# A two-block transformer kernel on one core: the second attention's output with values stationary, its softmax division folded into the head norm

## What is computed

```python
scores = jnp.where(valid, scores + bias, -jnp.inf)
probs = jax.nn.softmax(scores, axis=-1)
out = jnp.einsum('bhcqk,bhckd->bhcqd', probs, vb)
...
y = group_rmsnorm(jnp.concatenate([y_sb, y_ch, y_cv], axis=-1), out_norm_w[l])
x = x + y @ w_out[l]

def group_rmsnorm(y, w):
    yg = y.astype(jnp.float32).reshape(b, s, N_OUT_GROUPS, HEAD_DIM)
    yg = yg * lax.rsqrt(jnp.mean(yg * yg, axis=-1, keepdims=True) + EPS)
    return (yg.reshape(b, s, D_MIX) * w.astype(jnp.float32)).astype(y.dtype)
```

## Time and profile before

| what | value |
|---|---|
| median of 3 runs | 691.27 us (691.0 to 691.66) |
| profiled execution, whole | 691.82 us |
| its span, first to last instruction | 689.9 us |
| TensorE busy | 682.8 us (99%) |
| VectorE busy | 485.6 us (70%) |
| ScalarE busy | 416.6 us (60%) |
| GpSimd busy | 90.7 us (13%) |
| mean granted TensorE clock | 0.997 of full |

### The profile page before, as it was taken

The page is one execution under the profiler, slowest core; times in us unless marked ns, Lnnn a source line. Parts: engine busy times, 40 slices in busy tenths (PEclk is TensorE's granted clock), DMA queues, the critical chain, the costliest instruction groups (busy, mean ns, idle before and its releaser), DMA issues.

```text
span 689.9 us, 9453 instructions
## 1 busy us (share of the span) xinstructions
PE 682.8 (99%) x3796; PEld 587.5 (85%) x3796; DVE 485.6 (70%) x739; ACT 416.6 (60%) x705; POOL 90.7 (13%) x164
## 2 busy tenths in 40 slices
PE   9999999999999999999999999999999999999996
PEld 8888888888888888888888988888888888888885
DVE  6878796767666666667465767777868877777774
ACT  7787775656555555546555866665567665555553
POOL 2122020688100000012700000000000000000001
PEclk9999999999999999999999999999999999999998
DMA  9936534736555555536434335554453565555401
GB/s 336 392 132 229 198 123 160 266 133 243 187 188 190 204 198 194 183 131 225 175 134 161 123 123 201 195 194 179 161 207 146 218 209 182 183 185 187 179 0 62
DMA packets 19484, 126.14 MB, mean 183 GB/s; under 512 B 2416, under 2 KB 2544, under 8 KB 5232
## 3 DMA queue, kind: packets, MB, share of 16 engines
q1 hardware_dynamic: 19296, 125.34, 49.9%
q10 hardware_dynamic: 144, 0.20, 0.1%
HBM read 124.48 MB, written 1.05 MB: 182 GB/s over the span
## 4 chain that ended last, share of the span: by engine, by line
PE 99%; DVE 0%; issue 0%; ACT 0%; POOLq 0%; POOL 0%
PE bank L222 96%; PE bank L231 3%; DVE xres L243 0%; POOLq L1572 0%; DVE last L243 0%; ACT last L234 0%; ACT junk L234 0%; POOL ss L248 0%; POOL ones L267 0%; POOL half L267 0%; POOLq L151 0%; POOLq L1640 0%
## 5 line engine op out<-in xcount | busy, mean ns | idle before, releaser
L243 DVE TENSOR_TENSOR wlo<-raw,whi 128x1024 fp32r<-128x1024 f32 x222 | 271.6, 1235 | 61.5 <-ACT whi L234 58.4
L234 ACT ACTIVATE whi<-raw 128x1024 fp32r<-128x1024 f32 x222 | 230.3, 1051 | 5.7 <-PE bank L222 3.8
L222 PE MATMUL bank<-xb,whi 128*128 128x512 f32 x496 | 124.2, 392 | 0.0
L222 PE MATMUL bank<-xa,whi 128*128 128x512 f32 x432 | 108.2, 392 | 0.0
L222 PEld LDWEIGHTS bank<-xb,whi 128*128 128x128 f32 x496 | 90.4, 188 | 17.4 <-DVE sg L243 0.2
L222 PE MATMUL bank<-whi,xb 128*128 128x512 f32 (+1 forms) x352 | 96.0, 355 | 0.0
L222 PEld LDWEIGHTS bank<-xa,whi 128*128 128x128 f32 x432 | 78.9, 188 | 15.5
L222 PEld LDWEIGHTS bank<-xb,wlo 128*128 128x128 f32 x496 | 67.7, 190 | 4.9
L222 PEld LDWEIGHTS bank<-whi,xb 128*128 128x128 f32 x352 | 62.1, 189 | 9.3 <-ACT vtok L234 0.3
L222 PE MATMUL bank<-xb,wlo 128*128 128x256 f32 x496 | 69.1, 282 | 0.0
L222 PEld LDWEIGHTS bank<-xa,wlo 128*128 128x128 f32 x432 | 58.9, 190 | 4.2
(11 more groups left out here) (263 smaller groups left out, 930.1 us busy)
## 6 DMA issues: line engine op xcount, KB each, us to landing
raw<-in_w_dram SPq DMA_DIRECT2D x109, 1024.0 KB, 4.8
first<-in_first_dram SPq DMA_DIRECT2D x8, 388.0 KB, 6.8
raw<-in_w_dram SPq DMA_DIRECT2D x4, 512.0 KB, 9.6
bias<-in_bias_dram SPq DMA_DIRECT2D x1, 1024.0 KB, 8.9
xres<-in_x_dram SPq DMA_DIRECT2D x1, 1024.0 KB, 8.1
gain<-in_ffn_norm_w_dram SPq DMA_DIRECT2D x1, 512.0 KB, 8.9
gain<-in_mix_norm_g_dram SPq DMA_DIRECT2D x1, 512.0 KB, 9.6
gain<-in_ffn_norm_g_dram SPq DMA_DIRECT2D x1, 512.0 KB, 4.8
```

Source lines behind the costliest of these rows:

```text
L222: return P(lambda e: e.matmul(o, l, r, start=start, stop=stop), *w, inc=inc)
L234: return A(lambda e: e.activation(o, i, f, **kw), *w)
L243: return q(lambda e: e.tensor_tensor(out=o, in0=a, in1=b, op=op), *w)
```

## The change

`ch_out` now takes a pair of heads at once: the values of a head are stationary (64 columns), the transposed weights move (256 columns for key block 0, 128 for key block 1), and the two heads write the lower and the upper 64 partitions of the bank. The result has features on partitions. It isn't divided by `den` any more. `finish` and `ch_finish` are gone; both groups use `feature_norm`.

Since the undivided output is `den` times the true one, its norm is the same if EPS is replaced by EPS times `den` squared. So `ch_den_squares` makes `den2` = EPS * den * den on VectorE, `ch_den_rows` transposes it on TensorE (two transposes to 8 rows of 256 tokens), splits it into `den_h` and `den_l`, and `ch_den_sums` adds it into the bank of the squared sums by matmuls with a selection matrix `sel_r` of eight rows, which GpSimd writes once during the first attention. The logarithm then has no bias. `ch_probs` transposes its three blocks in another order.

```diff
+    den2 = N("den2", [128, 16])
+    den_h, den_l = [at(va_at + 1024 * i, f"den{p}", [8, 256], F32R) for i, p in enumerate("hl")]
+    sel, sel_r = at(qta_at, "sel", [8, 512]), at(sbmask_at, "sel_r", [8, 512], F32R)
...
-    def feature_norm(y, ybank, kt, ytoks, sbank, f, hl, z, *free):
+    def feature_norm(y, ybank, kt, ytoks, sbank, f, hl, z, *free, more=None):
...
-            mm(pb[sbank][:, :], blk_r[:, :], l[:, :], False, True)
+            mm(pb[sbank][:, :], blk_r[:, :], l[:, :], False, more is None)
+            if more:
+                more()
...
     def ch_out(h):
-        bank, pt, c, o = 2 + h // 4, wk[4 + h % 4], slice(h * 64, h * 64 + 64), (h % 4) * 64
-        o0, o1 = pb[bank][:, o:o + 64], pb[bank][:, 256 + o:256 + o + 64]
-        mm(o1, pt[:, 0:128], vb[:, 0, c], True, False, ch["pT", h], *ch["v"], *bank_free[bank])
-        mm(o1, pt[:, 128:256], vb[:, 1, c], False, True)
-        ch["out", h] = [mm(o0, pt[:, 256:384], vb[:, 0, c], True, True, inc=True)]
...
+        bank, c0 = 2 + h // 4, 256 * (h // 2 % 2)
+        for k in range(2):
+            for i in range(2):
+                v, pt = vb[:, k, (h + i) * 64:(h + i) * 64 + 64], wk[4 + (h + i) % 4]
+                mm(pb[bank][64 * i:64 * i + 64, c0 + 128 * k:c0 + 256], v, pt[:, 256 * k:256 + 128 * k], k == 0, k == 1,
+                   ch["pT", h + i], *ch["v"], *bank_free[bank])
+        ch["out", h] = ch["out", h + 1] = [P.mark()]
+
+    def ch_den_squares():
+        d = den[:, :].rearrange("p (g t h) -> p g t h", g=2, t=2)
+        o = den2[:, :].rearrange("p (t g h) -> p g t h", g=2, t=2)
+        for g in range(2):
+            ch["den"] = stt(o[:, g], d[:, g], EPS, d[:, g], ALU.mult, ALU.mult, ch["e", 7])
+
+    def ch_den_rows():
+
+        P.wait(ch["den"], *bank_free[4])
+        for t in range(2):
+            tr(pb[4][0:8, t * 128:t * 128 + 128], den2[:, 8 * t:8 * t + 8])
+        p = P.mark()
+        a = copy(den_h[:, :], pb[4][0:8, 0:256], p)
+        v = low(den_l[:, :], pb[4][0:8, 0:256], den_h[:, :], a)
+        bank_free[4] = [v]
+        ch["den rows"] = [a, v]
+
+    def ch_den_sums(g, bank):
+        P.wait(*ch["den rows"], sel_tok)
+        for i in range(2):
+            s, o = sel_r[:, (2 * g + i) * 128:(2 * g + i) * 128 + 128], pb[bank][:, 256 * i:256 * i + 256]
+            mm(o, s, den_h[:, :], False, False)
+            mm(o, s, den_l[:, :], False, i == 1)
...
+    later(ch_den_squares)
     conv_taps(1)
     conv_unit(4)
+    ch_den_rows()
     ch_out(4)
-    ch_out(5)
...
     conv_unit(5)
-    ch_scaled_0()
     ch_out(6)
-    ch_out(7)
-    ch_roots, ch_scaled_1, ch_finish_1 = ch_finish(1)
-    later(ch_roots)
-
+    sums_0()
+    later(scaled_0)
+    later(split_0)
...
+    def other_squares():
+        squares_1(*ch["sums 0"])
+        cv_squares()
+    ch["sums 0"] = [P.mark()]
+    later(other_squares)
     for k in range(KT - HOLD):
         u, lh, ll, w = mix_1(k)
         out_unit(u, (0, 1), lh, ll, k == 0, False, *w)
         release(u)
-        if k == 0:
-            ch_finish_0()
-        elif k == 1:
+        if k == 1:
+            sums_1()
             cv_sums()
-            ch_scaled_1()
-            later(cv_scaled)
-            later(cv_split)
-        elif k == 2:
-            ch_finish_1()
+            for fn in (scaled_1, split_1, cv_scaled, cv_split):
+                later(fn)
```

More of the change, by code:

```diff
@@ L526, in two_block_program @@
     qa = N("qa", [128, 2, 512])
+    va_at = N.lo
     va = N("va", [128, 2, 256])
@@ L538, in two_block_program @@
     bias = N("bias", [128, 8, 256])
+    sbmask_at = N.lo
     sbmask = N("sbmask", [128, 3, 128])
@@ L562, in two_block_program @@
     den = N("den", [128, 16])
-    rden = N("rden", [128, 16])
+    den2 = N("den2", [128, 16])
+    den_h, den_l = [at(va_at + 1024 * i, f"den{p}", [8, 256], F32R) for i, p in enumerate("hl")]
+    sel, sel_r = at(qta_at, "sel", [8, 512]), at(sbmask_at, "sel_r", [8, 512], F32R)
     cva = at(qb_at, "cva", [128, 2, 256])
@@ L700, in sb_out, with squares @@
         sb["out", 2 * b] = sb["out", 2 * b + 1] = [P.mark()]
-    def feature_norm(y, ybank, kt, ytoks, sbank, f, hl, z, *free):
+    def feature_norm(y, ybank, kt, ytoks, sbank, f, hl, z, *free, more=None):
         (h, l), parts, summed, v = hl, [], [], []
-        def squares():
+        def squares(*read):
             a = act(f, y, ACT.Square, *ytoks, *free, scale=0.125)
-            parts.append(copy(h[:, :], f, a))
+            parts.append(copy(h[:, :], f, a, *read))
             parts.append(low(l[:, :], f, h[:, :], parts[0]))
@@ L712, in sums @@
             mm(pb[sbank][:, :], blk_r[:, :], h[:, :], True, False)
-            mm(pb[sbank][:, :], blk_r[:, :], l[:, :], False, True)
+            mm(pb[sbank][:, :], blk_r[:, :], l[:, :], False, more is None)
+            if more:
+                more()
             summed.append(P.mark())
         def scaled():
-            a = act(f, pb[sbank][:, :], ACT.Ln, *summed, eps_tok, bias=eps[:, 0:1])
+            a = act(f, pb[sbank][:, :], ACT.Ln, *summed, eps_tok, **({} if more else {"bias": eps[:, 0:1]}))
             bank_free[sbank] = [a]
@@ L732, in feature_norm @@
         return squares, sums, scaled, split
-    finishes = [0]
     sq_free, ytok = {0: [], 1: []}, {}
[L738 to L771, removed]
     ch = {}
@@ L827, in ch_probs @@
         P.wait(ch["e", h], *bank_free[bank])
-        for i in range(3):
-            tr(pb[bank][:, i * 128:i * 128 + 128], s[:, i * 128:i * 128 + 128])
+        for c, i in enumerate((2, 0, 1)):
+            tr(pb[bank][:, c * 128:c * 128 + 128], s[:, i * 128:i * 128 + 128])
         p = P.mark()
@@ L835, in ch_out @@
     def ch_out(h):
-        bank, pt, c, o = 2 + h // 4, wk[4 + h % 4], slice(h * 64, h * 64 + 64), (h % 4) * 64
-        o0, o1 = pb[bank][:, o:o + 64], pb[bank][:, 256 + o:256 + o + 64]
-        mm(o1, pt[:, 0:128], vb[:, 0, c], True, False, ch["pT", h], *ch["v"], *bank_free[bank])
-        mm(o1, pt[:, 128:256], vb[:, 1, c], False, True)
-        ch["out", h] = [mm(o0, pt[:, 256:384], vb[:, 0, c], True, True, inc=True)]
-    def ch_finish(g):
-        v = V(lambda e: e.reciprocal(rden[:, g * 8:g * 8 + 8], den[:, g * 8:g * 8 + 8]), ch["e", 4 * g + 3])
-        return finish(2 + g, 2 + 2 * g, ch["out", 4 * g + 3][0], 8 * g, v)
+        bank, c0 = 2 + h // 4, 256 * (h // 2 % 2)
[25 more added lines that the diff above has]
+            mm(o, s, den_l[:, :], False, i == 1)
     cv = {}
@@ L957, in two_block_program @@
             sb_squares()
+            g = memset(sel[:, :], 0.0, P.mark())
+            g = select(sel[:, :].rearrange("p (j d) -> p j d", d=64), [[-1, 8], [0, 64]], ALU.not_equal, 1.0, 0, 1, g)
+            sel_tok = G(lambda e: e.tensor_copy(sel_r[:, :], sel[:, :]), g)
         elif n == 2:
@@ L982, in two_block_program @@
     ch_out(0)
-    ch_out(1)
     ch_probs(2)
@@ L989, in two_block_program @@
     ch_out(2)
-    ch_out(3)
-    ch_roots, ch_scaled_0, ch_finish_0 = ch_finish(0)
-    later(ch_roots)
+    squares_0, sums_0, scaled_0, split_0 = feature_norm(
+        pb[2][:, :], 2, 2, ch["out", 2], 0, sq[0][:, :], sb_hl, yt[0][:, :], *sq_free[0], more=lambda: ch_den_sums(0, 0))
+    later(squares_0)
     ch_probs(4)
@@ L1003, in two_block_program @@
     conv_unit(5)
-    ch_scaled_0()
     ch_out(6)
-    ch_out(7)
-    ch_roots, ch_scaled_1, ch_finish_1 = ch_finish(1)
-    later(ch_roots)
+    sums_0()
+    later(scaled_0)
+    later(split_0)
+    squares_1, sums_1, scaled_1, split_1 = feature_norm(
+        pb[3][:, :], 3, 4, ch["out", 6], 0, sq[1][:, :], sb_hl, yt[1][:, :], *sq_free[1], more=lambda: ch_den_sums(1, 0))
     cv_squares, cv_sums, cv_scaled, cv_split = feature_norm(
-        flat(cvy[:, :, :]), None, 6, [cv["out"]], 0, cvf[:, :], cv_hl, flat(cvy[:, :, :]))
-    later(cv_squares)
+        flat(cvy[:, :, :]), None, 6, [cv["out"]], 1, cvf[:, :], cv_hl, flat(cvy[:, :, :]))
     us = next_units(KT)
```

## The result

| | median | lowest to highest | runs |
|---|---|---|---|
| before | 691.22 us | 691.0 to 691.66 | 6 |
| changed | 696.52 us | 696.03 to 698.05 | 6 |

The ratio is 1.0079, with a 95% interval of 1.0069 to 1.0089: 5.3 us slower. The forecast was 694.3, the range 693.0 to 697.3. The profiled execution of the changed kernel took 697.27 us (span 694.4) against 691.82 (span 689.9).

What follows compares the result with a forecast made beforehand. TensorE, 99% of the span, was taken as the bound. Work -6.01 + 5.27, stall 3.4, convolution wait 0.05 and held units 0.35 gave +3.06 us, so 694.3 us from the median of 691.27; range 693.0 to 697.3.

Steps and rivals of the forecast that it cites:

- the case that it stood for: Main forecast, chance 0.68: stall behind `conv_unit(4)` without a clock fall, 694.3 us.
- the forecast's own bounds: Main case's limits: 693.3 (work -1.0, stall 3.0, tail 0) to 696.8 us (work +0.2, stall 4.3, tail 1.0).
- the clock case: Rival, chance 0.12: the stall behind `conv_unit(4)` brings back TensorE's half rate, adding 3.0 us, 697.3 us.
- the prediction's own signs of being wrong: `den2` on VectorE before 88 us, `ch_out` over 1.2 us a pair, or 512-column matmuls behind the gap over 0.4 apart.
- The new wait: TensorE behind `conv_unit(4)` waits for VectorE's `den2`: a stall of 3.4 us, ends 3.0 and 4.3.
- The three microseconds of the earlier trace: At kernel start, 6 us of matmuls at the lower clock would be 3 less at full speed; priced the clock rival.
- The work of TensorE: Across the second attention and its norms: 6.01 us removed, 5.27 added, 0.74 gained, between 1.0 gained and 0.2 lost.
- What is late next: Norms behind the second attention: group 0 hidden, group 1 with 0.25 us to spare, the convolution's squares 0.05 us of waiting.
- The held units: Weight units on VectorE ahead of the residual sum delay TensorE's transposes of `xn`: 0.35 us added, ends 0 and 1.0.
- the long chain of sizes: Operations priced by size (0.6 to 0.72, 0.95, 1.13 us) put VectorE free 0.6 us after the residual sum could begin.
- That the wait is hidden: Rival: VectorE has the squared sums ready before `conv_unit(4)` ends, 690.9 us; chance 0.08 together with half the stall gone.
- The tail: Rival, chance 0.12: norms and held units each fall short if ScalarE runs 0.6 later, about 1.2 more, 695.5 us.

Runs made afterwards that it cites:

- the second profile: Changed kernel measured once more, unedited, beside the other runs: 696.73 us, ratio 1.0073 to the kernel before.
- the version without a gap: Changed kernel with `den2`'s two small operations ahead of VectorE's weight unit and their transposes behind head 7's probabilities: 692.16 us against 691.46 for the kernel before.
- the eight runs of the kernel before with a gap of 2.3 or 2.9 us: Kernel before plus one TensorE wait behind `conv_unit(4)`, for VectorE's row sum (696.59 us) or the weight unit's remainder (696.12 us), four runs each.
- the first profile: Profiled execution of the changed kernel from its first measurement: 697.27 us, against 691.82 for the kernel before.
- The version with 128 rows: Version without a gap, its selection matrix and transposed squared sums filled with zeros to 128 rows: 691.67 us against 691.71 for the kernel before.
- the version without constants: Version without a gap, less squared sums of exponentials, their matmuls and selection matrix, EPS added undivided: 690.66 us against 691.71 for the kernel before.
- the two moves that hide it: Changed kernel with the small `den2` operations moved earlier on VectorE and their transposes later on TensorE: 692.16 us against 691.46 for the kernel before.

## Why the prediction was right or wrong

The direction, the cause and its place were right: the time rose because TensorE waits behind `conv_unit(4)` for two tiny operations that stand deep in VectorE's queue. The range held the time. The point was 2.2 us low, and the case that it stood for was not the one that came. That the range held the time is in part luck: the forecast's own bounds reach 696.5 only with a stall near 4.3 us and a tail near 1.0, and neither came; the upper end was the clock case's, at about twice what the clock cost. Two of the prediction's own signs of being wrong showed, both by the clock: a pair of heads took 1.48 us, over 1.2, and in the second profile the matmuls of 512 columns behind the gap started 0.42 apart (3.39 us for eight), over 0.4.

**The new wait: right, 2.96 for 3.4 us.** The next work could have started 1.04 us behind 86.25, as it did in the version without a gap (85.95 to 86.99), so at 87.29; it started at 90.25. In this execution the second attention began 0.51 us earlier (68.02 for 68.53). Counted from there, VectorE's side came as reckoned: TensorE starts at 90.76 for 90.8. TensorE was free at 87.80 for 87.45, as each pair of heads saved 0.36 and not 0.48, and the matmuls ahead of the third pair end 0.08 later (below).

**The clock: the chosen case was the wrong one.** It was a rival at 0.12 and came in both profiles of the changed kernel; of the eight runs of the kernel before with a gap of 2.3 or 2.9 us only one was without it, by its time. The reason held against it, that matmuls stand right up to the gap and right behind it, was no reason. Its price was also wrong, 3.0 against 1.4 and 1.5. In the first profile the pair took 1.48 for 0.80, the transposes of weights 1.20 for 0.71 and the eight matmuls behind them 1.97 for 1.93, each against the version without a gap, and the transposes of `den2` 0.52 for the 0.32 of the second profile, where the clock was full: 1.4 together. In the second profile the eight matmuls took 3.39 for 1.93 and the transposes 0.75 for 0.71. The transposes of `den2` themselves take 0.2 more at this place at full clock than in the version without a gap (0.32 for 0.14), which is not the clock's.

The three microseconds of the earlier trace rows were those of a start out of rest, read from the distances between matmuls alone: the profile's granted clock stands at 1.00 in that stretch of the kernel before, from 0 to 9 us. The Trainium skill's advice (TensorE: Matmul & The Clock Gate, Why this matters for your kernels) against idle gaps, which it gives for longer ones, was borne out here at 2.9 us, and in the kernel before one of 2.3 us was enough.

**The work of TensorE: the step that failed by its sign.** It was reckoned at 0.74 us gained, and the version without a gap is 0.70 us slower (interval 0.3 to 1.5). Two terms were off.
- The pair of heads took the 0.80 us of the earlier trace rows. But the 256-column matmuls ahead of it end later: 85.95 to 86.99 is 1.04, where 87.45 to 88.41 is 0.96. That is 0.08 four times, and 0.04 in the transposes behind three of the pairs: about 0.45 us in all. The distance of the block alone didn't show what changes at its edge.
- The constants were reckoned from the 256-column row at 0.96 and 0.2, and cost 1.75 us by the medians. By the distances in the version without a gap they cost 1.94: from the second matmul of the squared sums to the second of the next unit are 1.32 us (92.75 to 94.07), against 0.46 (92.55 to 93.01) without the constants, so 0.86 for a group (the second has the same 1.32), and the transposes of `den2` add 0.22 (87.79 to 88.64 against 87.81 to 88.44). Inside a group the matmuls did start 0.11 to 0.12 apart behind the first, which took 0.22. What was missing is about 0.1 us at each change between eight rows and 128. The version with 128 rows has 0.11 to 0.12 throughout. So the row's price was right for a matmul of full height, and wrong for the small one that seemed cheaper. The rule of the Trainium skill on weight loads (TensorE: Matmul & The Clock Gate, LDWEIGHTS), that rows don't matter, agrees with the spacing inside the group and doesn't speak of its edges.

With these two the sum for the work is -0.74 + 0.45 + 0.78 = +0.49 us.

**What is late next: the convolution's and group 1's norms.** Right that nothing stalls there. In the changed kernel the profile lists no wait of TensorE behind the gap. How little was to spare shows in the version without constants, which gets there earlier and waits 0.33 us for the convolution's squares.

**The held units: wrong, 0 for 0.35 us.** VectorE's residual sum and TensorE's transposes in the changed kernel, against the earlier trace rows:

```profile
112.64 3.50 DVE L243 TENSOR_TENSOR wlo<-raw,whi 128x1024 fp32r<-128x1024 f32 x3 [0.26 <-ACT whi L234]
116.35 1.37 DVE L243 TENSOR_TENSOR xres<-bank,xres 128x512 f32<-128x512 f32 x2 [0.21 <-PE bank L222]
119.60 1.42 DVE L251 SCALAR_TENSOR_TENSOR xn<-xres,rstd,gain 128x512 f32<-128x512 f32 x2 [1.88 <-POOL rstd L243]
```

The lead of VectorE over the sum shrank from 2.2 us to 0.21, so the change did push its queue that far; it was reckoned to be 0.6 on the other side. The version without a gap has the same 0.21, so the gap isn't what used the lead up. The sum still waited for TensorE, and 116.35 to the transposes at 120.92 is 4.57, as before (4.56). VectorE was free some 0.8 us earlier than the long chain of sizes said. The logarithm without its bias took 0.60 to 0.63 on ScalarE, where that with a bias took 0.72 in the kernel before, but no run isolates which sizes made up the 0.8.

**The sum again, with what was measured:** 0.70 for the work, 2.96 for the gap, 0.2 for the place of the `den2` transposes and 1.4 for the clock is 5.3 us, the measured difference. The profiles bear it out stage by stage. From the first score matmul of the second attention to the transposes of `xn` the kernel before takes 47.83 us (68.53 to 116.36), the changed one 52.90 (68.02 to 120.92), the version without a gap 48.37 (67.71 to 116.08): 5.07 more, and 0.54 more. From there to TensorE's last instruction the three take 567.56, 567.54 and 567.55, so nothing of the difference lies behind this stage. Ahead of it the profiles of all the kernels here differ by up to 1.1 us (67.71 to 68.83), which is why a difference of some tenths is better read inside the stage.

**The rivals.** That the wait is hidden was rightly held unlikely; the two moves that hide it give 692.16 beside 691.46 for the kernel before, where its own price said 690.9 beside 691.27, short by the same mistake in the work. The tail didn't wait at all.

## What to carry to other kernels

Where TensorE is busy 99% of the time, ask of every new operand which engine makes it and what stands ahead of it in that engine's queue: 0.15 us of work at the end of a queue that ran late, behind pieces that nobody was waiting for, cost 4.6 us. A gap on TensorE costs its length and can cost the clock behind it as well, so the case with the lower clock belongs in the forecast and not beside it. Price a small matmul by its neighbours too: a change of shape had an edge of 0.1 us on either side, and the same matmul padded with zeros to full height was cheaper.

## What the runs showed of the hardware that was not expected

- A pause of TensorE of 2.3 us between dense matmuls was followed by 1.2 GHz, and one of 1.26 us was not. Behind 2.92 us three of four runs had it and one had not, by their times; one of the three was profiled. The fall cost 1.4 and 1.5 us in two profiles of the changed kernel and 1.73 in the kernel before, at either length of gap.
- With the same gap the low stretch had begun by the first matmul behind it in one profile (0.53 granted from 90 to 92), and began about 1.6 us later in another (0.56 granted from 92 to 94, full before).
- Matmuls with eight rows of weights between matmuls with 128 cost about 0.1 us more at each change: 0.33 us against 0.24 ahead of the first, 0.22 against 0.11 behind it, 0.21 against 0.12 behind the last. The same matmuls with 128 rows cost none of that.
